# Holding the third split buffer for one more weight piece, and moving its two gather rows to the end of the ring

## The reference, cut to what matters

```python
q = jnp.einsum('td,dhk->thk', xc, w_query)                 # 1024 x 2048 weights
s = jnp.einsum('thpk,hpnk->thpn', q, sub_keys)             # 16 x 128 scores per token
top_s, top_i = lax.top_k(s, PEER_TOPK)
...
best_s, best_pos = lax.top_k(cand_s, PEER_TOPK)
idx = jnp.take_along_axis(cand_i, best_pos, axis=-1)
u = jnp.take(expert_u, idx, axis=0)
v = jnp.take(expert_v, idx, axis=0)
act = jax.nn.gelu(jnp.einsum('td,thkd->thk', xc, u))
return jnp.einsum('thk,thkd->td', (g * act).astype(v.dtype), v)
```

## Time and profile before

| | |
|---|---|
| median of 3 runs | 1375.24 us (1374.72 to 1376.69) |
| profiled execution | 1371.77 us, its span 1370.0 us |
| PE busy | 1162.6 us (85% of the span) |
| DVE busy | 970.5 us (71%) |
| ACT, POOL busy | 568.6 us, 571.7 us (42% each) |
| DMA | 374.44 MB, 273 GB/s over the span |
| of this the gathers' queue (q0) | 268.45 MB, 46.8% of the 16 engines' span |
| mean granted TensorE clock | 0.97 of full |

### The profile page before, as it was taken

The page is one execution under the profiler, slowest core; times in us unless marked ns, Lnnn a source line. Parts: engine busy times, 40 slices in busy tenths (PEclk is TensorE's granted clock), DMA queues, the critical chain, the costliest instruction groups (busy, mean ns, idle before and its releaser), DMA issues.

```text
span 1370.0 us, 16633 instructions
## 1 busy us (share of the span) xinstructions
PE 1162.6 (85%) x6104; PEld 827.7 (60%) x6104; DVE 970.5 (71%) x1937; ACT 568.6 (42%) x1026; POOL 571.7 (42%) x576
## 2 busy tenths in 40 slices
PE   5999899999999998985877888888887777778787
PEld 5999798899999988974863443334432222223222
DVE  4488888895577655556668877778777777777554
ACT  5376656664445434785423323333222222222221
POOL 0099999999700000000023444444444444444431
PEclk9999999999999999996999999999999999999999
DMA  6644334344536544520349999999999999999995
GB/s 221 201 142 138 109 124 124 123 154 158 181 124 215 196 164 136 175 92 31 124 162 419 425 421 426 427 426 427 426 415 426 425 410 414 423 413 415 425 427 248
DMA packets 137332, 374.44 MB, mean 273 GB/s; under 512 B 6817, under 2 KB 103073, under 8 KB 104353
## 3 DMA queue, kind: packets, MB, share of 16 engines
q0 software_dynamic: 36864, 268.45, 46.8%
q1 hardware_dynamic: 98048, 99.62, 22.3%
q10 hardware_dynamic: 2336, 5.29, 1.1%
HBM read 372.29 MB, written 1.05 MB: 273 GB/s over the span
## 4 chain that ended last, share of the span: by engine, by line
PE 35%; DMA 28%; DVE 23%; issue 7%; ACT 6%; ACTq 0%; POOL 0%; POOLq 0%; DVEq 0%
PE unit L375 26%; DMA row<-in_experts,big 24%; PE unit L600 6%; DVE w_lo L1144 4%; DMA conv_in<-in_experts,big 3%; DVE conv_acc L1159 3%; DVE work L1487 3%; ACT w_hi L692 1%; ACT probs L925 1%; DVE big L1411 1%; ACT probs L792 1%; DVE probs L1287 1%; DVE big L1244 1%; DVE big L1420 1%; DVE big L1417 1%
## 5 line engine op out<-in xcount | busy, mean ns | idle before, releaser
L375 PE MATMUL unit<-in_hi,w_hi 128*128 128x256 f32 x1216 | 377.7, 311 | 14.2 <-DVE w_lo L1144 9.4
L1800 POOL DMA_INDIRECT row<-in_experts,big x128 | 141.5, 1106 | 539.2 <-DVE big L1480 334.1
L375 PE MATMUL unit<-in_lo,w_hi 128*128 128x256 f32 x1216 | 347.7, 286 | 0.0
L375 PE MATMUL unit<-in_hi,w_lo 128*128 128x256 f32 x1216 | 347.4, 286 | 0.0
L600 PE MATMUL unit<-row,probs 128*128 128x512 f32 x512 | 252.9, 625 | 71.9 <-ACT probs L925 71.4
L1144 DVE TENSOR_TENSOR w_lo<-w_raw,w_hi 128x2048 fp32r<-128x2048 f32 x94 | 218.8, 2331 | 112.8 <-ACT w_hi L692 112.8
L925 ACT ACTIVATE probs<-ident,big 128x128 f32<-128x128 f32 x256 | 102.8, 401 | 460.4 <-DVE big L1499 460.4
L375 PEld LDWEIGHTS unit<-in_hi,w_hi 128*128 128x128 f32 x1216 | 237.6, 195 | 32.9 <-issue 21.2
L375 PEld LDWEIGHTS unit<-in_lo,w_hi 128*128 128x128 f32 x1216 | 237.4, 195 | 16.1 <-issue 16.0
L375 PEld LDWEIGHTS unit<-in_hi,w_lo 128*128 128x128 f32 x1216 | 237.0, 195 | 0.0
L692 ACT CAST w_hi<-w_raw 128x2048 fp32r<-128x2048 f32 x94 | 176.9, 1898 | 120.9 <-PE unit L375 65.1
(11 more groups left out here) (242 smaller groups left out, 1396.1 us busy)
## 6 DMA issues: line engine op xcount, KB each, us to landing
w_raw<-in_w_in SPq DMA_DIRECT2D x58, 1024.0 KB, 5.2
w_raw<-in_w_mem_kv SPq DMA_DIRECT2D x8, 1024.0 KB, 5.3
w_raw<-in_w_out SPq DMA_DIRECT2D x8, 1024.0 KB, 5.1
w_raw<-in_w_query SPq DMA_DIRECT2D x8, 1024.0 KB, 5.4
w_raw<-in_w_diff_proj SPq DMA_DIRECT2D x4, 1024.0 KB, 6.4
w_raw<-in_w_x_proj SPq DMA_DIRECT2D x4, 1024.0 KB, 5.2
w_raw<-in_w_conv_proj SPq DMA_DIRECT2D x4, 1024.0 KB, 5.3
big<-in_x ACTq DMA_DIRECT2D x2, 1024.0 KB, 7.9
```

Source lines behind the costliest of these rows:

```text
L375: m = e.matmul(unit[:, to:to + 256], fixed, moving, start=start, stop=stop)
L1800: e.indirect_dma_start(out=UV.ap(g), out_offset=None, in_=experts, in_offset=bass.IndirectOffsetOnAxis(ap=expert[t][:, n:n + 1], axis=0)). ...
```

## The change

Three things change. Pieces 88 and 89 still take their split buffers in the ring's turn, so piece 89 goes into `w2` (last used by piece 86) and not into `w0` (last used by piece 87). `hi(89)` and `lo(89)` stand directly behind `hi(88)` and `lo(88)`, ahead of the query copies on ACT and ahead of `choose(0)` on DVE. And since `w2` is now in use until piece 89 is done, its two rows, `row0` and `row1`, come last among the eight, with a wait on that piece.

```diff
@@ -318,11 +318,13 @@
         for p in range(PIECES_ALL):
-            split.take(p, None if p < FIRST_UNDER else 1 - (p - FIRST_UNDER) % 2)
+            split.take(p, None if p < FIRST_UNDER + 2 else (p - FIRST_UNDER) % 2)
         early_space.close()
         rows = [sb(f"row{i}", [2 * D])[:, :] for i in range(4)]
-        rows += [big[2][:, :], big[0][:, :], big[1][:, :], flat(conv_in[:, :, :])[:, 0:2 * D]]
-        ROW_FREE = [("piece", FIRST_UNDER - 2)] * 4 + [("x2", 1)] * 3 + [("h3", 1)]
+        rows = [*rows[2:], big[2][:, :], big[0][:, :], big[1][:, :],
+                flat(conv_in[:, :, :])[:, 0:2 * D], *rows[:2]]
+        ROW_FREE = ([("pair free", "mix")] * 2 + [("x2", 1)] * 3 + [("h3", 1)]
+                    + [("piece", FIRST_UNDER + 1)] * 2)
@@ -1111,9 +1113,9 @@
             hi(FIRST_UNDER)
+            hi(FIRST_UNDER + 1)
             queries_copy(0)
             score_copies(0)
-            hi(FIRST_UNDER + 1)
             choose_exp(0)
@@ -1748,9 +1750,9 @@
             lo(FIRST_UNDER)
+            lo(FIRST_UNDER + 1)
             for _ in choose(0):
                 pass
-            lo(FIRST_UNDER + 1)
             for _ in choose(1):
                 pass
```

## The result

| | before | changed |
|---|---|---|
| median | 1375.24 us (1374.72 to 1376.69, 5 runs) | 1367.99 us (1366.17 to 1369.03, 5 runs) |
| ratio | | 0.9948, 95% interval 0.9937 to 0.9958 |
| profiled execution, its span | 1371.77 us, 1370.0 us | 1369.03 us, 1367.3 us |
| PE, DVE, ACT busy | 1162.6, 970.5, 568.6 us | 1159.9, 970.5, 568.8 us |
| DMA | 374.44 MB | 374.43 MB |

The bytes and DVE's and ACT's work are the same. The profiled execution of before lies 3.5 us under the median of its runs, so the two profiles show only 2.7 us of the 7.25. Where the rest is became a question of its own.

What follows compares the result with a forecast made beforehand. The gather stream's fixed DMA rate was taken to bound the second half. Its first packet 4.0 us earlier, less 0.4 for a slow start, gave 3.6 off the 1375.24 median: 1371.6 us, 8-in-10 range 1370.0 to 1374.6.

Steps and rivals of the forecast that it cites:

- The bound: Second half, 256 gathers at a fixed DMA rate (410 to 427 GB/s): only the stream's start, bytes or dry time count.
- `hi(89)` and `lo(89)` at no price: Made early on ACT and DVE, both lie in idle time with 4.0 and 3.7 us to spare; price 0.
- The first gather: POOL's first gather instruction, without a subtraction beside it, takes 0.94 us instead of 2.99 and ends 2.05 us earlier.
- The delay behind it: From POOL's instruction end to q0's first packet: 1.5 us instead of 3.4 without the load of piece 91; bounds 1.1 and 3.4.
- The slow start: Gather stream starting without a load beside it loses 0.4 us at first; bounds 0 and 0.8.
- DVE's seam: Without lo(89) between the choices, choose(1) starts 2.19 us earlier and the first dot product 3.7 to 3.8 us earlier.
- the ring: First six gathers use places already free; gather 6 waits for piece 89 with 6 us of cover; price 0.
- the one on PE: Piece 89 follows directly, second queries come 8.5 us earlier; worth nothing by itself, since DVE idles only 1.55 us for them.
- Does the stream stay fed?: Gather stream starts 3.6 us earlier, the row-freeing chain 3.7 us earlier, so the pattern moves as a whole, q0's pause included.
- the fixed delay: Rival: 3.0 to 3.4 us is the gathers' own delay, so only POOL's lock is gained; 1373.0 to 1373.6 us; chance 0.24.
- nothing moves: Rival: the first gather's 2.99 us is a cold start and the delay fixed; 1375.2 us, give or take 0.3; chance 0.12.
- the wait of `hi(89)`: Slower rival: hi(89) on ACT, awaiting piece 86, holds up the query copies from 4.0 us of lateness; about 1378; chance 0.06.

Runs made afterwards that it cites:

- e4: Changed kernel with one two-input 128x2048 subtraction, output unused, put between choose(0) and choose(1), the load staying early; 1371.4 us, 0.9986 to the kernel before.
- e3: Changed kernel with the load of piece 91 held until head 0 is chosen, no subtraction beside it; 1370.17 us, 0.9981 to the kernel before.
- e6: Kernel before with the load of piece 91 held back until the first value has been added; 1373.04 us, 1.0002.
- e1: Kernel before without edit, profiled and timed again; 1371.84 us, 0.9997.
- the first measurement: First timing of both kernels, the one in the result table; 1375.24 us before, 1367.99 us changed, ratio 0.9948.
- The occasions at 1372: Later timings of the unedited changed kernel where the kernel before is near 1372 us; ratios 0.9970, 0.9961, 0.9969, 0.9972.
- e13: Kernel before with ACT's first copy of the second queries repeated six times, each waiting for the last; 1375.68 us, 1.0026.
- e14: Kernel before with ACT's first copy of the second queries repeated twelve times, each waiting for the last; 1378.84 us, 1.0058.
- e11: Kernel before without edit, on an occasion when it is near 1375 us; 1374.47 us, profiled execution 1375.35 us.
- e15: Changed kernel with ACT's first copy of the second queries repeated twelve times, each waiting for the last; 1370.32 us, 0.9990 to the kernel before.

## Why the prediction was right and wrong

**The bound** was right: no engine's busy time changed by more than 3 us, and the time followed the stream's start and length in each experiment.

**`hi(89)` and `lo(89)` at no price**: right. They lie in idle time, with 3.80 us left on ACT and 3.93 on DVE (forecast 4.0 and 3.7).

**The first gather**: right, 1.84 us gained (2.99 to 1.15; forecast 2.05), and e4 shows that the subtraction makes the difference.

**The delay behind it** was the disputed term. The mechanism holds: a load in flow keeps the new gather back (e3 with it, e6 without it). The size was off. I took 1.5 us, with a lower bound of 1.1 from the load that had no traffic beside it; measured, a gather without traffic has its first packet after 0.7 us (e4, e6, all six profiles of the changed kernel). The term is 3.46 - 0.70 = 2.8 us and not 1.9. Counted from the start of POOL's instruction the first packet came 4.6 us earlier (6.45 us behind it before, 1.85 now), which is past the 4.4 us that I gave as the most, at a chance of 0.02.

**The slow start** costs more than I took. From 707.77 on, the windows at 74, 205 and 377 GB/s lack 0.06 + 0.52 + 0.12 us of a stream at 427, and those up to 716 (393 and 397 GB/s) another 0.44: 1.1 us, not 0.4. The pause at 744 did not stay but closed (411 GB/s from 743 to 746), worth some 0.2 us. The stream is accordingly 0.2 to 1.2 us longer than the 648.0 of e1, and in the two profiles of the first measurement 0.7 us longer (649.0 against 648.3).

With 0.7 us for the longer stream, the sum of these is 1.84 + 2.76 - 0.7 = 3.9 us, against 3.6. The start and the slow start were both too small, by 0.6 and 0.3 us, and the sum came near in part because these errors are of opposite sign. The occasions at 1372 show 4.3, 5.3, 3.7 and 4.7 us. Up to here the forecast was right in kind and somewhat low in size.

**DVE's seam and the ring**: right. Counted from the first gather, the first dot product comes 3.9 us earlier (forecast 3.7 to 3.8), and in the changed kernel the first eight gathers follow each other on POOL with 0.3 us between them, so piece 89 keeps none of them back.

**The step that failed** is the one on PE: "By itself this gives nothing: what waits for it is the exponentials of head 1 and through them DVE, with 1.55 us of idle time". It put the 8.5 us by which the second queries come earlier at nothing. I read a wait of 1.55 us as a small cost, when it meant that the chain from the second queries to DVE had no cover at all. Whatever comes late on it makes DVE late by as much and by PE's slower scores on top, and gather 8 with it; behind gather 8 some 2 us are absorbed, and the rest goes into the stream (e13: 3.7 us for 3.67, e14: 6.9 for 7.37). With it failed "Does the stream stay fed?", which I asked of the changed kernel only. On two of seven occasions the kernel before was 2.6 and 3.2 us above the mean of the other five (1372.1). The profile of one of these shows ACT's copy 3 us late and the stream dry, and e13 shows that a lateness somewhat above this (5.4 us on DVE, where e11 has 4.6) costs 3.7 us. In the changed kernel ACT's wait before that copy was 4.44 to 4.47 us in all six profiles, there are 4.8 us of cover behind it (e15), and its time did not move. So some 4 of the 7.25 us are the earlier start, which is shown. The other 3 are most likely a stall of the kernel before that the changed kernel does not have; for the first measurement itself that is inferred.

The low end of 1370.0 was set by the scatter of the median and 4.4 us of gain, and held none of this. It was also too near because I subtracted from the median of 1375.24 what I had read in a profile at 1371.77. The 3.5 us between them were a finding to explain, not an offset to carry along. From that profile the same sum gave 1368.2 us, and the changed kernel measured 1367.99; with terms that miss in both directions, some of that nearness is luck.

**Not shown**: what released ACT in e11, and why only on some occasions. The five timed executions of the first measurement (1374.7 to 1376.7 us) were not profiled, and the one that was, at 1371.77, does not show the stall. That their 3 us have the same cause rests on e11, on the like size, and on e13; no run has both the lateness of e11 and the changed kernel. The rivals: the fixed delay fell with e3 and e6, "nothing moves" with e4, and the wait of `hi(89)` never reached its 4.0 us.

## What to carry to other kernels

Where half of a kernel runs at a fixed transfer rate, look at what stands in the two microseconds before its first packet: a two-input vector operation beside the issuing instruction and a load in flow were worth 4 us here, and neither stood out in any engine's busy time. A short wait that remains on a chain that feeds such a stream is a sign that the chain has no cover up to that wait; put the work early enough that the wait is gone, even if the wait itself is worth nothing. And when the median lies several microseconds off the profiled execution, first find out what the other executions do, since a change may remove just that.

## What the runs showed of the hardware

- A gather that comes new to q0 while q1 is in full flow had no packet for 3.0 us (e3) to 3.5 us (the kernel before), until the load was nearly through; once both flow they alternate, 197 to 197 packets. The Trainium skill, "DMA: Bandwidth & Descriptors", section "Queues, rings and completion order", has the queues take turns packet by packet. The second case agrees with it, the first does not.
- Without other traffic the first packet of a gather came 0.7 us behind the end of POOL's instruction (e4, e6, the changed kernel). The Trainium skill, "DMA: Bandwidth & Descriptors", section "Latency and other measured facts", gives about 1 us for a software-generated DMA; the runs show less, if one counts from that end.
- The first gather took 2.99 us in each profile with the subtraction behind `choose(0)`, and 1.15 us in each without it, where later ones take 0.94. "SBUF — State Buffer" of the Trainium skill, section "Who interferes with whom", names the exclusion that this agrees with.
- PE, after 3.6 to 8 us without work, made the same 16 score matmuls in 3.59 to 3.78 us at a granted clock of 0.50 to 0.51, where they took 2.05 us after 0.7 us without work (e11, e13, e14, e15 against e1).
- A stream with few gathers queued slows down before it runs dry: 336 GB/s over 12 us in e15, without a gap in q0.
- Identical code had two levels of time by occasion, about 1372 and 1375 us, on one and the same chip.
